# A hybrid mLSTM and mixture-of-experts block: the last two tiles' normed rows made on ScalarE and GpSimd, the routing table's products merged, and the unread products dropped

## What is computed

```python
def hybrid_layer(x, ...):
    hn = rms_norm(x, norm_mix)
    proj = hn @ w_in + b_in                      # q, k, v, o, gates, conv channels
    y_m = sigmoid(o) * mlstm_chunkwise(q, k, v, log_i, log_f)
    y_c = short_gated_conv(cb, cc, cx, conv_w)
    x = x + concatenate([y_m, y_c]) @ w_out      # the residual rows, "x2" in the kernel
    hn2 = rms_norm(x, norm_ffn)                  # the normed rows
    # top-1 of 4 groups, then top-2 of its 8 experts, for each token
    # each expert: (silu(h @ w_gate) * (h @ w_up)) @ w_down, weighted and added to x
    return x + hier_moe(hn2, ...)
out = rms_norm(hybrid_layer(x, ...), norm_final)
```

## Time and profile before

| | us |
|---|---|
| median of 3 runs | 1828.26 |
| lowest and highest | 1827.84, 1829.36 |
| profiled execution, its own time | 1829.41 |
| its span in the trace | 1827.7 |
| mean granted clock of TensorE | 0.997 |
| PE busy | 1807.3 |
| DVE busy | 824.4 |
| POOL busy | 588.9 |
| ACT busy | 292.8 |

### The profile page before, as it was taken

One profiled execution on the slowest core, in us unless ns is written; L12 is line 12 of the kernel. 1 busy time (PEld: TensorE's weight loads), 2 busy tenths in 40 slices (PEclk: granted clock), 3 DMA queues, 4 the chain that ended last, 5 costly groups with the idle time before them and its releaser, 6 DMA issues.

```text
span 1827.7 us, 28959 instructions
## 1 busy us (share of the span) xinstructions
PE 1807.3 (99%) x10499; PEld 1453.7 (80%) x10499; DVE 824.4 (45%) x1772; ACT 292.8 (16%) x732; POOL 588.9 (32%) x668
## 2 busy tenths in 40 slices
PE   9999999999999999999999999999999999999997
PEld 8888668888478886688884877788888888888875
DVE  5556755476652767554764761522212212212221
ACT  2022120211211211202111111111111111111111
POOL 5933212044130234120440223234333333333332
PEclk9999999999999999999999999999999999999998
DMA  7642722314522326223133498888888888888874
GB/s 300 225 164 70 267 103 93 127 70 162 184 93 80 141 70 235 112 93 124 73 139 140 156 364 306 325 339 331 329 316 330 316 333 307 333 328 328 330 287 162
DMA packets 81712, 392.30 MB, mean 215 GB/s; under 512 B 17707, under 2 KB 18003, under 8 KB 48784
## 3 DMA queue, kind: packets, MB, share of 16 engines
q1 hardware_dynamic: 50576, 310.49, 45.9%
q0 software_dynamic: 25632, 58.90, 8.7%
q10 hardware_dynamic: 5360, 21.03, 2.9%
HBM read 356.10 MB, written 60.86 MB: 228 GB/s over the span
## 4 chain that ended last, share of the span: by engine, by line
PE 93%; POOL 3%; issue 1%; DMA 1%; DVE 1%; ACT 0%; POOLq 0%; SPq 0%; DVEq 0%; ACTq 0%
PE ps_proj L701 24%; PE ps_proj L1121 6%; PE ps_proj L1123 6%; PE ps_proj L730 6%; PE ps_state L1142 6%; PE ps_num L1142 6%; PE ps_proj L742 5%; PE ps_rows L1121 3%; PE ps_scores L1123 3%; PE ps_rows L1123 3%; PE ps_scores L1121 3%; PE ps_scores L730 3%; PE ps_proj L763 2%; PE ps_num L1149 2%; PE ps_state L730 2%; PE ps_num L1052 1%
## 5 line engine op out<-in xcount | busy, mean ns | idle before, releaser
L1121 PE MATMUL ps_proj<-hnT,wo 128*128 128x128 f32 (+3 forms) x992 | 201.2, 284 | 0.0
L1123 PE MATMUL ps_proj<-hnT,wo 128*128 128x128 f32 (+3 forms) x992 | 199.4, 283 | 0.0
L1121 PEld LDWEIGHTS ps_proj<-hnT,wo 128*128 128x128 f32 x992 | 154.6, 191 | 13.6 <-issue 13.6
L1123 PEld LDWEIGHTS ps_proj<-hnT,wo 128*128 128x128 f32 x992 | 153.9, 191 | 0.0
L701 PE MATMUL ps_proj<-hnT,ww 128*128 128x256 f32 x640 | 151.6, 380 | 0.0
L701 PEld LDWEIGHTS ps_proj<-hnT,ww 128*128 128x128 f32 x640 | 119.3, 190 | 16.8 <-issue 1.4
L1537 POOL TENSOR_TENSOR xres<-ww 128x512 f32<-128x512 f32 x12 | 15.2, 1267 | 291.9 <-DMA ww<-in_w_slots 274.3
L1121 PE MATMUL ps_scores<-hnT,wo 128*128 128x128 f32 (+3 forms) x496 | 99.7, 283 | 0.0
L1123 PE MATMUL ps_rows<-hnT,wo 128*128 128x128 f32 (+3 forms) x496 | 99.7, 283 | 0.0
L1123 PE MATMUL ps_scores<-hnT,wo 128*128 128x128 f32 (+3 forms) x496 | 99.7, 283 | 0.0
L1121 PE MATMUL ps_rows<-hnT,wo 128*128 128x128 f32 (+3 forms) x496 | 99.7, 283 | 0.0
(11 more groups left out here) (516 smaller groups left out, 3558.2 us busy)
## 6 DMA issues: line engine op xcount, KB each, us to landing
wo<-in_w_gu SPq DMA_DIRECT2D x128, 1024.0 KB, 7.2
ww<-in_w_slots SPq DMA_DIRECT2D x43, 1024.0 KB, 4.8
og<-in_w_dn SPq DMA_DIRECT2D x32, 1024.0 KB, 4.9
vx<-in_w_dn SPq DMA_DIRECT2D x32, 1024.0 KB, 7.5
xin<-in_x SPq DMA_DIRECT2D x16, 512.0 KB, 6.2
ww<-w_v_sums SPq DMA_DIRECT2D x16, 512.0 KB, 3.4
xres<-in_x SPq DMA_DIRECT2D x16, 512.0 KB, 6.0
x_rows<-x ACTq DMA_DIRECT2D x16, 512.0 KB, 5.1
```

What stands on the lines that cost most here:

```text
L1121: pe.matmul(GU[m][:, 0:n_], wo[:, kt, m * P:(m + 1) * P], xT[:, kt, 0:n_], start=(kt == 0), stop=(kt == KT - 1), skip_group_check=True)
L1123: mm = pe.matmul(GU[m][:, CAP:CAP + n_], wo[:, kt, FF + m * P:FF + (m + 1) * P], xT[:, kt, 0:n_], start=False, stop=(kt == KT - 1), skip_g ...
```

## The change

1. All 19 unread products are dropped.
2. The slots stored by the earlier batches enter the table in one step. `stored_slots` now writes codes and weights into one bank, in two products of 64 columns; before, there were two of 32 columns for the codes (in `out_part`) and two for the weights (in the passage). The weights no longer use `ps_scores`.
3. The last half of the table is made in one go (`late_table`): 8 products of 64 columns in place of 8 of 32 columns for the codes and, after another stretch of gate and up products, 8 for the weights. The early half keeps its two parts.
4. DVE no longer makes the normed rows of tiles 14 and 15. ACT multiplies `x2` by the scale (`scaled_rows`), and POOL multiplies by `gffn` in two instructions over 128x1024, behind item 0's gather.
5. ACT squares tile 15 before it copies that tile's turned rows, not after, and makes `scaled_rows(0)` between them; `scaled_rows(1)` comes behind the copy of the last logits.
6. DVE makes the last half's weights before its places and one-hot rows, and sums up the comparison of the experts (`rank_e`) after it has read the table.

```diff
+            def late_table():
+
+                pe.wait_ge(S_("table_rows_ready"), 4)
+                for n in range(2 * TL):
+                    if n == TL:
+                        pe.wait_ge(S_("hot_ready"), 2)
+                    mm = half_products(1, n, slice(0, 2 * NE))
                 mm.then_inc(S_("table_turned"), 1)
...
             router_logits(NTILE - 2, CT - 2)
             pe.wait_ge(S_("out_read"), out_read(NB - 1, 1, "c12"))
-            unread(2)
             router_rows(NTILE - 2)
-            half_table(0)
+            early_tokens()
             router_turn(NB - 1, CT - 1)
-            unread(3)
             router_logits(NTILE - 1, CT - 1)
-            unread(2)
             router_rows(NTILE - 1)
-            half_weights(0)
+            early_weights()
...
                     if kt == FIRST_TABLE:
-                        half_table(1)
-                    if kt == FIRST_TABLE + 1:
-                        half_weights(1)
+                        late_table()
...
-            unread(12)
             main_transposes(0)
             half_ranks(1)
             first_gate_up()
...
+                def scaled_rows(i):
+                    act.wait_ge(S_("rs2_ready"), NTILE + i)
+                    act.wait_ge(S_("ss2_ready"), NTILE + i)
+                    own_instruction(act)
+                    act.activation(hn2[i][:], x2[i][:], ACT.Copy, scale=st2[:, i, 1:2]).then_inc(S_("ss2_ready"), 1)
...
                 store_residual(3)
+                squares_of(3)
                 with act.If(b > NB - 2):
+                    scaled_rows(0)
                     router_act(NTILE - 1)
                     own_instruction(act)
-                squares_of(3)
...
                     logits_turned(NTILE - 1)
+                    scaled_rows(1)
                     store_rows(2)
...
             gather_main(idx[:, 0:1])
+            for i in range(2):
+                pool.wait_ge(S_("ss2_ready"), NTILE + i + 1)
+                pool.wait_ge(S_("hn2_ready"), NTILE - 2 + i)
+                pool.tensor_tensor(hn2[i][:], hn2[i][:], gffn, ALU.mult).then_inc(S_("hn2_ready"), 1)
...
                     early.rows_weight()
-                    normed_rows(2)
...
             last.rows_token()
+            last.weights()
+            last.rows_weight()
             last.place()
             last.one_hot()
-            last.weights()
-            last.rows_weight()
-            dve.wait_ge(S_("hn2_stored1"), 16 * (2 * (NB - 1) + 1))
-            dve.wait_ge(S_("rs2_ready"), NTILE + 1)
-            dve.scalar_tensor_tensor(out=hn2[1][:], in0=x2[1], scalar=st2[:, 1, 1:2], in1=gffn, op0=ALU.mult,
-                                     op1=ALU.mult).then_inc(S_("hn2_ready"), 1)
...
-            then(dve.tensor_reduce(rank_e.unsqueeze(2), perm3, AX.X, ALU.add))
             dve.wait_ge(S_("table_turned"), TABLES["whole"])
...
             dve.sem_inc(S_("items_made"), 1)
+            then(dve.tensor_reduce(rank_e.unsqueeze(2), perm3, AX.X, ALU.add))
             second_item()
```

More of the change, by code:

```diff
@@ L274, in build @@
         ITEMS = {"main_rows": 1, "items": 2, "weights": 3, "second": 4, "order": 5, "sorted": 6, "visits": 7, "overflow": 8}
-        TABLES = {"early": 1, "whole": 3, "weights": 4}
+        TABLES = {"early": 1, "whole": 3, "early_weights": 2}
         gfin = ww[1][:, 0:D]
@@ L854, in _, with stored_slots @@
             TABLE = STA[:, 1, :]
[L856 to L862, removed]
+            def stored_slots():
                 pe.wait_ge(S_("slots_loaded"), 16 * (1 + TQ))
                 pe.wait_ge(S_("out_read"), out_read(NB - 1, 1, "u3"))
-                stored_slots(0, TABLE)
@@ L868, in half_products @@
-            def half_products(i, n, o, bank):
-                first = (2 * TL * i + n) * 2 * NE + o * NE
+                for i, part_ in enumerate((slots_main, slots_tail)):
+                    pe.matmul(TABLE[:, 2 * NE * i:2 * NE * (i + 1)].rearrange("p (o e) -> p o e", o=2), ident[:],
+                              part_[:].rearrange("p e o -> p o e"), start=(i == 0), stop=False, skip_group_check=True)
+            def half_products(i, n, cols_):
+                first = (2 * TL * i + n) * 2 * NE
@@ L870, in half_products @@
                 for part_, at in enumerate((slice(0, P), slice(P, SLOTS))):
-                    mm = pe.matmul(bank[:, part_ * NE:(part_ + 1) * NE], hot_half[i][:, n // TL, n % TL, at],
-                                   tok_w[:, first:first + NE], start=False, stop=(n == 2 * TL - 1), skip_group_check=True)
-                return mm
-            def half_table(i):
+                    to = 2 * NE * part_
+                    mm = pe.matmul(TABLE[:, to + cols_.start:to + cols_.stop], hot_half[i][:, n // TL, n % TL, at],
+                                   tok_w[:, first + cols_.start:first + cols_.stop],
+                                   start=False, stop=(n == 2 * TL - 1), skip_group_check=True)
@@ L1015, in _ @@
                         elif p == 1 and i == 4 and b == NB - 1:
-                            out_part(b, p, i, OUT_BANK[bank], new, {1: stored_codes, 2: lambda: router_turn(NB - 1, CT - 2)})
+                            out_part(b, p, i, OUT_BANK[bank], new, {1: stored_slots, 2: lambda: router_turn(NB - 1, CT - 2)})
                         else:
@@ L2693, in _ @@
                                    ALU.is_gt))
-            then(dve.tensor_reduce(rank_e.unsqueeze(2), perm3, AX.X, ALU.add))
             dve.wait_ge(S_("table_turned"), TABLES["whole"])
-            then(dve.tensor_copy(tail_c[:, 0:1], STA[:, 1, NE:NE + 1]))
+            then(dve.tensor_copy(tail_c[:, 0:1], STA[:, 1, 2 * NE:2 * NE + 1]))
             decoded(none4[:, 0:1], tail_c[:, 0:1], 1, pad[:, 1:2], other[:, 0:1])
@@ L2700, in _ @@
             then(dve.tensor_copy(main_e, STA[:, 1, 0:NE]))
-            then(dve.tensor_copy(tail_e, STA[:, 1, NE:2 * NE]))
-            dve.wait_ge(S_("table_turned"), TABLES["weights"])
-            then(dve.tensor_copy(wgt_e, SC[:, 0:NE]))
-            then(dve.tensor_copy(wgt4_e, SC[:, NE:2 * NE]))
+            then(dve.tensor_copy(tail_e, STA[:, 1, 2 * NE:3 * NE]))
+            then(dve.tensor_copy(wgt_e, STA[:, 1, NE:2 * NE]))
+            then(dve.tensor_copy(wgt4_e, STA[:, 1, 3 * NE:4 * NE]))
             dve.sem_inc(S_("items_made"), 1)
+            then(dve.tensor_reduce(rank_e.unsqueeze(2), perm3, AX.X, ALU.add))
             second_item()
```

20 lines of the change are left out of this document (8 added, 12 removed).

## The result

| | before | after |
|---|---|---|
| median of 19 runs each, us | 1828.94 | 1831.62 |
| lowest and highest | 1827.75, 1830.81 | 1830.91, 1835.54 |
| profiled execution, its own time | 1829.41 | 1831.44 |
| its span | 1827.7 | 1829.8 |
| mean granted clock | 0.997 | 0.994 |

The changed kernel takes 1.0016 times as long, with a 95% interval of 1.0010 to 1.0022; the medians are 2.7 us apart. That is within the 0.2% that the prediction called no change, at its upper half; the forecast was +2.4 us.

A forecast was written before the change was run, and what follows sets the result against it. PE, nearly always busy, was taken to bound the kernel, with DVE's chain setting item 0's gate start. Start +1.7, table -1.7, item 1 +0.6, clock +1.9, less 0.1, rounded to +2.4: 1830.7 us, range 1825.4 to 1832.8.

The forecast's parts named there:

- DVE held by POOL: Before item 0's counts, DVE's two-operand steps wait for POOL's two products to end; counts 2.5 us later, at 1032.0.
- The start of the gate: Item 0's gate products on PE start at about 1032.9, 1.7 us later than before.
- The merged table: In the gate stretch one table part of 8 products goes from PE's path: -1.7 us.
- cost by columns: Upper bound for the merged table in the gate stretch: a product costs by its columns, so the gain is 0.
- The clock: PE idles 4.5 us before item 0's gate products, which then start at 1.2 GHz; the return costs +1.9 us.
- Item 1: At item 1's down products PE waits for hidden values, as DVE falls 1.5 us back with 0.9 room: +0.6 us.
- The second gather: The second item's gather has 2.2 us of room before its transposes and keeps 0.7, so no wait.
- (a): Rival at the passage: DVE is held, but the clock stays up; +0.5 us, 1828.8 us, chance 0.18.
- (b): Rival at the counts: DVE is not held, gate products 1.5 us earlier; -2.6 us in all, 1825.7 us, chance 0.13.
- (d): Rival at the first gate products: 1.2 GHz lasts about twice as long; +4.3 us in all, 1832.6 us, chance 0.19.

The follow-up runs named there:

- e4: The changed kernel with POOL's two products waiting for DVE's counts and tile 14's store behind ACT's turned rows of item 0; 1.0001 times the kernel before.
- e12: The kernel before with the merged table's edits alone (items 2 and 3), the same program as e7 on another chip; 0.9989 times the kernel before.
- e9: e1 with 12 more unread products between item 0's transposes and the last half's counts; 1.0001 times the kernel before.
- e8: The kernel before with all 19 unread products taken out and nothing else changed; 1.0015 times the kernel before.
- e1: The changed kernel with all 19 unread products put back at their four places; 1.0019 times the kernel before.
- e6: The changed kernel with the sum of the comparison (rank_e) back ahead of the table's first read; 1.0020 times the kernel before.
- e7: The kernel before with the merged table's edits alone (items 2 and 3 of the change); 0.9991 times the kernel before.
- e5: e4 with unread products 2, 3, 2 and 5 put back and the sum rank_e ahead of the table's read; 1.0006 times the kernel before.
- e11: e5 with POOL's products behind the last one-hot rows, 9 unread products ahead of the transposes and 4 behind, replacing the 5; 1.0001 times the kernel before.
- e2: The changed kernel with only the 12 unread products ahead of item 0's transposes put back; 1.0006 times the kernel before.

## Why the prediction was right

**DVE held by POOL: right, and the main term.** Expected were ends of POOL's products at 1024.8 and 1027.4, and DVE steps of about 1 and over 2 us. They ended near 1024.1 and at 1026.54, which is 0.7 and 0.9 us earlier, as was the whole passage by 0.71; the steps took 1.22 and 2.24. e4 gives the cause by itself.

**The start of the gate: +1.7 forecast, +2.17 measured.** The counts came at 1031.22, which is 1031.93 on the clock of the run before: forecast 1032.0. The missing 0.5 is PE's part. The counts' products ran at the lower clock: from L847 to the gate 1.33 us, where it was 0.90. The prediction had put the whole of the clock's price behind the start of the gate.

**The merged table: -1.7 forecast, -1.79 measured** (e12). The upper bound, cost by columns, is out.

**The clock: +1.9 forecast, +1.83 measured at the gate** (the changed kernel against e9), and 0.4 more at the counts' products, above. The return price at the kernel's start was a good stand-in. The step that failed is where the clock falls. The prediction had the fall in the 4.5 us in front of the counts, and called the removed unread products "worth nothing by themselves". It fell at about 1023, before any long idle stretch: PE there had waited 1.44 us and then 0.53, where 5 of the 7 small unread products had been, and was working again when it fell. e8 shows the same in the kernel before: without the 19 its clock is at 0.91 from 1020 to 1024 and at 0.50 behind, and it loses 0.15%, 0.07 to 0.24. So removing the unread products has a price with or without POOL's products. The idle stretch for DVE has one too, with or without unread products (e1). In the changed kernel both pay for the same fall, and that is why one term of 1.9 gave the right sum. That the term came out right with the fall at another place and for another reason is luck.

**Item 1: +0.6 forecast, +0.51 measured,** but with another reason. The prediction laid it on DVE's falling behind PE as a whole, and said that moving the sum of the comparison "does not help", no more. e6 and e7, which differ from each other in nearly everything else and share the sum's old place, both have 25.79 us there. Taking the sum back is enough to remove the wait: the prediction overlooked that DVE would idle 3.99 us ahead of the read. The moved sum is not the only thing that can cause the wait: e5 has the sum in the old place and a wait of 0.30 us, with one-hot rows later.

**The second gather: 0.7 us of room forecast.** It starts at 1049.23 and lands 4.7 us later, at 1053.9, for transposes at 1054.52: 0.6 us.

**The rivals.** (a), the clock stays, is what e9 shows once the holes are filled: +0.2 us in ratio (known to 1.6 us) against its +0.5. (b), DVE not held, is e4 and e11 up to the counts; what was missing in (b) is that the counts' earlier time was partly paid again, with 0.59 us of waiting for the one-hot rows in e5 and 2.4 us for the tail's gather in e11. (d), a low stretch twice as long, did not come: the clock was back at 1036.5, some 4 us behind the first gate product.

## What to carry to other kernels

- When work moves to GpSimd, list which VectorE instructions with two SBUF operands can meet it, and add what is left of GpSimd's instruction to their chain, up to all of it; then look for a place where that chain has room, and see which transfer waits for the moved work in turn.
- Products that nobody reads paid here where they lay in the idle stretch just ahead of the work that counts (e9), or where the low stretch fell on them (e2). Moving the wait from one side of the transposes to the other left the old cover useless (e1), so check the granted clock window by window behind each wait, not only where the unread products stood.
- Run each part of a mixed change by itself: here one part (the merged table) was a gain of 0.11%, 0.02 to 0.20, and the rest of it lost 0.27% (1.0016 against 0.9989, from two chips, so an estimate).

## What was not expected of the hardware

- The hold of POOL and DVE goes both ways. In e11, DVE's step with two operands ran first, over 1037.26 to 1038.49, at its usual 1.23 us, and POOL's product that began at 1037.35 took 3.35 us in place of 2.35: 1.0 more, near the 1.14 that was left of DVE's. DVE's timeline of e11:

```profile
1035.07 2.16 DVE L2702 SCALAR_TENSOR_TENSOR yT<-total,kept_first 128x32 f32<-128x32 f32 x1
1037.26 1.23 DVE L2704 TENSOR_TENSOR yT<-yT 128x1024 f32<-128x1024 f32 x1
```

- The clock can fall while PE works. In e1 it stood at 1.00 through 3.19 idle microseconds and fell 1.7 us behind the restart; in the changed kernel it fell near 1022.8, 0.9 us after PE had taken up work again. The price then lies on useful work although the trace shows no low clock in the idle stretch.
- The same stretch in the same kernel can go either way (e7 and e12, idle 1.87 and 1.82 us). A profile of one execution shows one of the two.
